# Inverting the RWKV chunk matrices as 64 by 64 diagonal quarters: one transpose for two units, joins across the partition halves, and an untransposed last level

## The reference, cut to what matters

```python
def rwkv_step(s_state, inp):
    r, w, k, v, kk, a = inp
    sa = jnp.einsum('bhvk,bhk->bhv', s_state, -kk)
    s_new = (s_state * w[:, :, None, :] + sa[..., None] * (kk * a)[:, :, None, :]
             + v[..., None] * k[:, :, None, :])
    y = jnp.einsum('bhvk,bhk->bhv', s_new, r)
    return s_new, y
```

## Time and profile before

| | |
|---|---|
| runs | 2348.77, 2349.24, 2352.55 us, median 2349.24 |
| profiled execution: span | 2348.8 us |
| PE busy | 2298.1 us, 98% |
| DVE / ACT / POOL busy | 54% / 34% / 2% |
| TensorE clock granted, mean | 0.998 of full |

### The profile page before, as it was taken

One profiled execution on the slowest core, in us unless ns is written; L12 is line 12 of the kernel. 1 busy time (PEld: TensorE's weight loads), 2 busy tenths in 40 slices (PEclk: granted clock), 3 DMA queues, 4 the chain that ended last, 5 costly groups with the idle time before them and its releaser, 6 DMA issues.

```text
span 2348.8 us, 46080 instructions
## 1 busy us (share of the span) xinstructions
PE 2298.1 (98%) x19261; PEld 2219.6 (94%) x19261; DVE 1277.7 (54%) x1962; ACT 787.5 (34%) x1167; POOL 47.8 (2%) x71
## 2 busy tenths in 40 slices
PE   5999999999999999999999999999999999999998
PEld 5999999999999999989989989899999999999998
DVE  4444434487767767636526537355555654445354
ACT  5221221233333333324234233233333342335443
POOL 0000000000000000000000000000000000000000
PEclk9999999999999999999999999999999999999999
DMA  5312212133333344112112121142222244335365
GB/s 187 115 63 81 88 62 80 67 105 123 109 127 127 104 139 152 60 47 86 42 65 85 48 90 37 47 153 72 73 90 74 88 148 169 141 141 179 143 206 188
DMA packets 64151, 246.65 MB, mean 105 GB/s; under 512 B 8722, under 2 KB 16068, under 8 KB 45636
## 3 DMA queue, kind: packets, MB, share of 16 engines
q1 hardware_dynamic: 64020, 244.69, 30.0%
HBM read 214.49 MB, written 30.17 MB: 104 GB/s over the span
## 4 chain that ended last, share of the span: by engine, by line
PE 92%; DVE 3%; ACT 2%; DMA 2%; issue 1%; SPq 0%; DVEq 0%; POOL 0%; ACTq 0%; POOLq 0%
PE acc L941 55%; PE acc L1103 10%; PE acc L1472 6%; PE branch L1103 5%; PE branch L1197 2%; PE branch L1472 2%; PE branch L1235 2%; PE branch L1190 1%; PE branch L1380 1%; ACT w_hi L1519 1%; DMA scratch<-in_x_all 1%; PE branch L1048 0%; DVE act_lo L2745 0%; PE branch L1041 0%; PE branch L1025 0%
## 5 line engine op out<-in xcount | busy, mean ns | idle before, releaser
L941 PE MATMUL acc<-act_hi,w_hi 128*128 128x320 f32 (+3 forms) x3328 | 1016.8, 306 | 1.7 <-DVE act_lo L2745 1.5
L941 PE MATMUL acc<-act_lo,w_hi 128*128 128x320 f32 (+3 forms) x3328 | 986.1, 296 | 0.0
L941 PE MATMUL acc<-act_hi,w_lo 128*128 128x320 f32 (+3 forms) x3328 | 985.7, 296 | 0.0
L941 PEld LDWEIGHTS acc<-act_hi,w_hi 128*128 128x128 f32 x3328 | 626.9, 188 | 16.7 <-issue 4.6
L941 PEld LDWEIGHTS acc<-act_lo,w_hi 128*128 128x128 f32 x3328 | 627.1, 188 | 0.7
L941 PEld LDWEIGHTS acc<-act_hi,w_lo 128*128 128x128 f32 x3328 | 626.6, 188 | 0.0
L1979 DVE TENSOR_TENSOR w_lo<-w_raw,w_hi 128x2048 fp32r<-128x2048 f32 x135 | 309.1, 2290 | 273.2 <-ACT w_hi L1519 270.7
L1519 ACT ACTIVATE w_hi<-w_raw 128x2048 fp32r<-128x2048 f32 x135 | 258.6, 1916 | 164.7 <-PE branch L1472 126.8
L1472 PE MATMUL acc<-act_lo,w_hi 128*128 128x288 f32 x384 | 113.2, 295 | 0.0
L1472 PE MATMUL acc<-act_hi,w_hi 128*128 128x288 f32 x384 | 113.0, 294 | 0.0
L1472 PE MATMUL acc<-act_hi,w_lo 128*128 128x288 f32 x384 | 112.9, 294 | 0.0
(11 more groups left out here) (444 smaller groups left out, 3271.8 us busy)
## 6 DMA issues: line engine op xcount, KB each, us to landing
w_raw<-in_w_stream SPq DMA_DIRECT2D x136, 1024.0 KB, 4.8
w_raw<-in_w_stream SPq DMA_DIRECT2D x68, 512.0 KB, 5.8
gate_logits<-gate_out SPq DMA_DIRECT2D x48, 288.0 KB, 2.2
scratch<-gate_logits SPq DMA_DIRECT2D x48, 288.0 KB, 5.3
scratch<-in_x_all SPq DMA_DIRECT2D x9, 512.0 KB, 6.6
branch_rows<-branch_out SPq DMA_DIRECT2D x16, 288.0 KB, 2.2
scratch<-in_x_all SPq DMA_DIRECT2D x3, 1024.0 KB, 10.1
out_y_prompt<-scratch SPq DMA_DIRECT2D x6, 512.0 KB, 3.0
```

Of the source, the lines that this page charges most:

```text
L941: last = mm(acc[s][:, at:at + hi - lo], a[:, s, w], b[:, k, lo:hi], start=(k == order[0] and a is whi and b is xh), stop=(k == order[-1] a ...
```

## The change

- The inverse up to level 5 keeps only the diagonal quarters: `DD1` is now 64 columns for each unit (and an eleventh place that repeats unit 0), not 128.
- Level 0 is built in `EE0` (ten unit quarters made by POOL from a mask). Ten transposes in one stage (`turn_squares`, at block 18) turn two neighbouring units at a time; ACT picks both quarters' results out with five copies (`squares_out`).
- After levels 1 to 4 one transpose turns two units (`turn_pairs`: five transposes, not ten). The turned quarters lie crossed: the partition half says which unit of the pair, the columns say which quarter. So from level 2 on both joins cross the partition halves for half of their matmuls: `a_d` writes a unit's product to the half where the turned quarter lies, `d_a_d` brings it back. Both joins now write one stretch of 320 columns across two banks (`JOIN_AT`), so that DVE masks it in one instruction and subtracts it in two.
- The transposes stand ahead of au in the same stage. The semaphore from ACT's copy is waited for by DVE, ahead of low, and no longer by PE ahead of du.
- After level 5 ten transposes (again `turn_squares`) write the whole `DDT` by five copies; POOL has cleared `DDT` before. Level 6's du swaps its operands so that its result is already turned; DVE writes it negated into `DDT`. The transposes after level 6 are gone, and `solved` stands two blocks earlier in `plan`; what follows it keeps its blocks. Level 6's du stands one block later than before.

```diff
-                def join(lhs, rhs, step):
-                    for q in range(10):
-                        for m, r in enumerate(halves64):
-                            last = mm(bra[r, 512 * m + 32 * q:512 * m + 32 * q + 32], lhs[r, q, r], rhs(q, r), start=True, stop=True)
+                UNITS = ([(2 * j + m, m) for j in range(5) for m in range(2)]
+                         + [(2 * j + m, 1 - m) for j in range(5) for m in range(2)])
+                def place(q, m, crossed):
+                    half, n = (q % 2, 5 * m + q // 2) if crossed else (m, q)
+                    return halves64[half], n
+                def a_d(lv, crossed):
+                    for q, m in UNITS:
+                        r, (to, n) = halves64[m], place(q, m, crossed)
+                        first = DD1[r, q, :].rearrange("p (b two w) -> p b two w", two=2, w=1 << lv)[:, :, 0, :]
+                        last = mm(bra[to, JOIN_AT + 32 * n:JOIN_AT + 32 * n + 32], AT[r, q, r], first, start=True, stop=True)
+                    pt.done(last, f"au{lv}")
+                def d_a_d(lv, crossed):
+                    for q, m in UNITS:
+                        r, (at_, n) = halves64[m], place(q, m, crossed)
+                        d = DDP[at_, q // 2, r] if crossed else EE0[r, q, :]
+                        o = JOIN_AT + 160 * (q % 2) + 32 * (q // 2)
+                        last = mm(bra[r, o:o + 32], d, UU[at_, n, 0:32], start=True, stop=True)
+                    pt.done(last, f"du{lv}")
...
-                    pe.wait_ge(*vt.after(i, f"inv{lv - 1}"))
                     if lv == 1:
-                        pe.wait_ge(*vt.after(i, "w1"))
-                        pe.wait_ge(*at.after(i, "t0_1"))
+                        pe.wait_ge(*at.after(i, "t0"))
+                    else:
+                        pe.wait_ge(*vt.after(i, f"inv{lv - 1}"))
+                        if lv < LEVELS - 1:
+                            turn_pairs(lv - 1)
+                        else:
+                            turn_squares(DD1, lv - 1)
...
                     pe.wait_ge(*vt.after(i, f"low{lv}"))
-                    if lv > 1:
-                        pe.wait_ge(*at.after(i, f"t{lv - 1}_1"))
...
-                    pe.wait_ge(*at.after(i, "t6_1"))
+                    pe.wait_ge(*vt.after(i, "inv6"))
...
-                plan += [(block + 3, w1), (block + 5, lambda: turn_level(0, 0)), (block + 6, lambda: turn_level(0, 1))]
-                block += 1
-                block += 7
+                plan += [(block + 3, w1), (block + 5, turn_first)]
+                block += 8
                 for lv in range(1, LEVELS):
                     plan.append((block, lambda lv=lv: level_a_d(lv)))
-                    if lv > 1:
-                        plan += [(block, lambda lv=lv: turn_level(lv - 1, 0)), (block + 1, lambda lv=lv: turn_level(lv - 1, 1))]
-                    plan.append((block + 2, lambda lv=lv: level_d_a_d(lv)))
+                    plan.append((block + (2 if lv < LEVELS - 1 else 3), lambda lv=lv: level_d_a_d(lv)))
                     block += 4
-                plan += [(block, lambda: turn_level(6, 0)), (block + 1, lambda: turn_level(6, 1)), (block + 3, solved)]
+                plan += [(block + 1, solved)]
...
+                parts_of = bra[:, JOIN_AT:JOIN_AT + 320].rearrange("p (q n) -> p q n", q=10)
...
-                        for m, r in enumerate(halves64):
-                            last = tt(UU[r, :, 0:32], part(m, r), masks[r, at:at + 32].unsqueeze(1).to_broadcast([64, 10, 32]), ALU.mult)
+                        last = tt(UU[:, :, 0:32], parts_of, masks[:, at:at + 32].unsqueeze(1).to_broadcast([P, 10, 32]), ALU.mult)
...
-                each = ident.unsqueeze(1).to_broadcast([P, 10, P])
-                Q.done(g.tensor_tensor(DDT[:, :, :], each, each, ALU.mult), "unit_blocks")
+                each = masks[:, unit:unit + 64].unsqueeze(1).to_broadcast([P, 10, 64])
+                g.tensor_tensor(EE0[:, 0:10, :], each, each, ALU.mult)
+                Q.done(g.memset(DDT[:, :, :], 0.0), "unit_blocks")
```

More of the change, by code:

```diff
@@ L569, in build @@
         cv = Carver(x2)
-        DD1 = cv(1280, 10, 128)
+        DD1 = cv(704, 11, 64)
+        EE0 = cv(704, 11, 64)
+        DDP = EE0[:, 0:10, :].rearrange("p q n -> p (q n)").rearrange("p (j n) -> p j n", j=5)
         DDT = cv(1280, 10, 128)
         assert cv.at <= x3
+        JOIN_AT = 512 - 160
+        SLOTS = [(brb, P * k) for k in range(8)] + [(bra, 768), (bra, 896)]
         cv = Carver(x2)
@@ L1215, in level_d_a_d, with turn_pairs, turn_squares, turn_first @@
                     pe.wait_ge(*vt.after(i, f"low{lv}"))
-                    if lv > 1:
-                        pe.wait_ge(*at.after(i, f"t{lv - 1}_1"))
                     pe.sem_inc(joins_begun, 1)
                     if lv < LEVELS - 1:
-                        join(DDT, lambda q, r: UU[r, q, 0:32], f"du{lv}")
+                        d_a_d(lv, lv > 1)
                     else:
                         for j, (h, c) in enumerate(late):
-                            last = mm(bra[64:128, 512 + 64 * j:576 + 64 * j], DDT[64:128, 5 * h + c, 64:128], UU[64:128, j, :], start=True, stop=True)
+                            last = mm(bra[0:64, 64 * j:64 * j + 64], UU[64:128, j, :], DDT[64:128, 5 * h + c, 64:128], start=True, stop=True)
                         pt.done(last, f"du{lv}")
[L1226 to L1236, removed]
+                def turn_pairs(lv):
+                    for j in range(5):
+                        last = turn(brb[:, P * j:P * j + P], DD1[:, 2 * j:2 * j + 2, :].rearrange("p q n -> p (q n)"), ident)
+                    pt.done(last, f"turned{lv}")
+                def turn_squares(src, lv):
+                    for k, (bank, o) in enumerate(SLOTS):
+                        w = (k - 1) % 10
+                        last = turn(bank[:, o:o + P], src[:, w:w + 2, :].rearrange("p q n -> p (q n)"), ident)
+                    pt.done(last, f"turned{lv}")
+                def turn_first():
+                    pe.wait_ge(*vt.after(i, "w1"))
+                    turn_squares(EE0, 0)
                 def w1():
@@ L1786, in _, with squares_out, pairs_out @@
                 S.done(f(ybuf[:, :], cz, ACT.Exp, scale=-1.0), "z_exp")
[L1788 to L1795, removed]
+                def squares_out(dst, lv):
+                    for m, to, k in ((1, 0, 0), (1, 8, 8), (0, 0, 1), (0, 7, 8), (0, 9, 0)):
+                        bank, o = SLOTS[k]
+                        n = 2 if k == 8 else 8 if m else 7 if k else 1
+                        r = slice(64 * m, 64 * m + 64)
+                        src = bank[r, o:o + P * n].rearrange("p (q two s) -> p q two s", q=n, two=2)[:, :, m, :]
+                        last = f(dst(r, slice(to, to + n)), src, ACT.Copy)
+                    S.done(last, f"t{lv}")
+                def pairs_out(lv):
+                    act.wait_ge(*G.after(i, f"turned{lv}"))
+                    S.done(f(DDP[:, :, :].rearrange("p a b -> p (a b)"), brb[:, 0:5 * P], ACT.Copy), f"t{lv}")
+                act.wait_ge(*G.after(i, "turned0"))
+                squares_out(lambda r, qs: DD1[r, qs, :], 0)
                 act.wait_ge(gates_out[0], i * 32 + 16 * (ROW_STORES))
@@ L1803, in _ @@
                 split_hi(N(7))
-                for lv in range(4, LEVELS):
-                    other_side(lv)
+                pairs_out(4)
+                act.wait_ge(*G.after(i, "turned5"))
+                squares_out(lambda r, qs: DDT[r, qs, r], 5)
                 act.wait_ge(*G.after(i, "solved"))
```

53 lines of the change are left out of this document (31 added, 22 removed).

## The result

The changed kernel takes 2323.95 us (median of 4 runs, 2322.73 to 2325.12), the kernel before, on the same chip, 2349.01 us (4 runs, 2348.19 to 2352.55). The ratio is 0.9887, with an interval of 0.9873 to 0.9901: 23 to 30 us less. Carried over to the 2349.24 us that stand at the head, that is 2322.7 us. The forecast was 2327 in a range of 2323 to 2335.

A forecast was written before the change was run, and what follows sets the result against it. PE's list of work was taken as the time. Four steps gave 5.6 us a pass, 22.5 in four; 2348.8 less 22.5 plus 0.4 for level 3 is 2326.7, so 2327, range 2323 to 2335.

The forecast's parts named there:

- What bounds the kernel: PE, busy for 98% of the span, sets the time; the chain of waits never leaves it in the RWKV loop's first pass.
- Transposes: On PE, 160 transposes would remain in place of 280, at the same 0.11 us each.
- Step 1: Levels 2 to 5: second transposing stage gone, joins unchanged; a level 6.65 us in place of 7.57, 3.7 us less a pass.
- Steps 2 and 3: Level 6 with ten transposes in one stage, about 0.4 us less a pass; two transposing stages after it gone, 1.34 less.
- step 3: After level 6, two stages of five transposes go and nothing takes their place: 1.34 us less a pass.
- Step 4: Level 0: ten transposes in one stage, 1.10 us in place of 1.33, 0.2 us less a pass.
- DVE at level 3: Tightest margin: DVE's subtractions, reciprocal and masking end 0.15 us before PE's du3; 0.1 us a pass taken as cost.
- ACT, POOL: Copies after levels 0 to 4 and 6, and level 0's clearing of DDT, stay hidden behind PE; tightest quoted margin 0.4 us.
- A: Rival: au1's two partition halves in one PSUM bank cannot overlap; 4.9 us in all, time 2332; 9 in 100.
- B: Rival: crossed joins from level 2 on lose overlap; 24 to 49 us, time 2351 to 2375; 7 in 100.
- B's half: Only the 20 crossed instructions in each of 32 joins lose overlap: 24 us, the whole gain, 2351; 3 in 100.
- C: Rival: PE waits at low3, t0 and one or two others; 4 to 8 us in all, 2330 to 2335; 9 in 100.

The follow-up runs named there:

- turned_twice: The changed kernel with each of the five transposes of levels 2 to 5 done twice; 2331.23 us, ratio 0.9919.
- last_level_alone: The kernel before with only level 6's swapped operands and negated write into DDT, and the transposing stages after it gone; 2346.99 us, ratio 0.9990.
- four_in_turn: The changed kernel with the crossed joins' 20 matmuls reordered to take turns over all four quarters; 2312.73 us, ratio 0.9848.
- one_quarter_at_a_time: The changed kernel with the crossed joins ordered by quarter, five matmuls in one before the next; 2347.79 us, ratio 0.9997.
- changed_again: The changed kernel run once more, unaltered, for a second execution and ratio; 2323.5 us, ratio 0.9898.

## Where the prediction was right, and the step that failed

- **What bounds the kernel**: right. PE's list of work set the time, and all that left it left the time.
- **Transposes**: right. 160 remain, five of them in a row at 0.55 us, ten at 1.09 (predicted 1.10); turned_twice gives 0.11 us each on its own.
- **Step 1, levels 2 to 5**: this one failed. It says "Joins have as many matmuls, of the same size" and lets each keep its 1.28 us. The measured join is 1.08, since from level 2 on it uses four quarters and overlaps at the one change of pair: a term of zero where -0.20 us in each of 32 joins belongs, 6.4 us. That is the 6.65 against 6.28 us of a level, and it is what carried the time out of the range. I had the pair of numbers in my own rivals (72 ns for one quarter, 34 for two) and weighed them only for a loss; the same two rows say that a third and a fourth quarter could be a gain, though not how much.
- **Steps 2 and 3**: predicted 0.4 + 1.34 us, measured 1.64; last_level_alone shows step 3 by itself, 1.33. **Step 4**: 0.2, measured 0.2.
- **DVE at level 3**: 0.1 us a pass was taken, nothing came. Two subtractions took 0.56 us (0.68 by my working) and the masking 0.43 (0.50).
- **ACT, POOL**: five copies took 1.58 us (1.9 expected), the MEMSET of 1280 columns 1.17 (at most 1.55). All that was to stay hidden behind PE did. DVE's masking beside that MEMSET took 0.98 us for 640 columns; beside POOL's tensor operation it had been 1.57.
- **A** falls: au1, with both halves in one bank, takes 1.29 us. The Trainium skill, TensorEngine Tiling (Array Packing), Restrictions and Gotchas, has it that different row tiles can't access one PSUM bank at the same time; this trace shows no cost of it where the two outputs lie on different partition halves.
- **B** falls the other way: crossed joins overlap more. The same page of the Trainium skill, Key Properties, says that different tiles can load weights and multiply in parallel; four_in_turn agrees, 0.72 us in place of 1.28. Its price was real all the same: one_quarter_at_a_time loses overlap by the order of the list, 1.83 us a join, and stands at no change, near B's half.
- **C** falls: no wait of PE in these stages of the changed kernel.
- **The rest of the sum**: the merge stage's wait of 2.8 us became another one of 4.1, which nothing in my working had. And I took next to nothing to lie around the span, by setting the span of one execution beside the time of another. Where both numbers of one execution are known, the run is 1.9 to 2.0 us longer than the span in the changed kernel (2322.73 and 2320.7), and 1.8 to 3.5 us in the kernel before.

Together: the sum's 22.5 us and the joins' 6.4 are 28.9 in four passes, where 28.2 were measured. That the time still came within 0.3 us of the range is in part luck, since 2 to 4 us of those 28.2 don't reach the runs.

Open stay what makes PE wait at the end of a pass in last_level_alone and ahead of the merge stage in the changed kernel, with the instruction transfers as the likely reason, and where the rest of the passes' gain goes.

## What to carry to other kernels

Where small matmuls use quarters of the array, read the pace of one quarter and of two from the trace, and let neighbours in the list go to as many different quarters as there are: the order alone moved this kernel by 35 us, from 2347.8 to 2312.7. When a cost in a forecast is bounded from rows of one, two and more units at work, ask of the same rows what a gain would be, not only what a loss would be. A stage taken out of a loop should be looked at beyond itself, since a wait can come at another place: 1.67 us at the end of a pass in last_level_alone, 4.1 us ahead of the merge stage in the changed kernel.

## What had not been expected of the hardware

- A quarter of the array takes an instruction of a join every 56 to 58 ns, with two or four quarters at work: 40 instructions take 1.83 us in one quarter after another, 1.28 in two at a time, 0.72 in four. The overlap reaches only a little ahead: with twenty in one pair and then twenty in the other, only 0.20 us are saved at the change.
- Waits of PE that no engine is seen to cause: 1.67 us at the end of a pass, which six more matmuls make go away, and 3.7 to 4.4 us ahead of the merge stage, which 20 transposes at the start of the kernel make go away.
- The stretches of 3.4 us (6.8 in two of the traces) at a granted clock of 0.5 (1.2 GHz). In the changed kernel one comes right behind that wait of 4.1 us ahead of the merge stage. Windows of its trace:

```profile
1888.00:1891.70 3.70, 1.04 (x8) 1.07 (x9) 1.79 (x3) 3.47 (x7) 0.00 (x0) 1.00 0.25 60
1891.80:1895.20 3.40, 3.40 (x17) 3.40 (x16) 3.10 (x3) 1.28 (x1) 0.00 (x0) 0.50 0.98 335
```

PE was busy for 1.04 of 3.7 us, and then works through 3.4 us at half the clock. It doesn't come each time: in changed_again nothing of the kind follows the same wait of 3.7 us, and the stretch lies at 2103.6, behind another wait, of 1.8 us.
